# A causal 31-tap convolution stage: GpSimd makes the low halves of the weights, VectorE takes more taps

## The reference, cut to what matters

```python
def conformer_conv(x, w_in, b_in, conv_w, conv_b, ln_g, ln_b, w_out, b_out):
    a, g = jnp.split(x @ w_in + b_in, 2, axis=-1)
    h = a * jax.nn.sigmoid(g)
    h = lax.conv_general_dilated(
        h, conv_w[:, None, :], window_strides=(1,),
        padding=[(CONV_KERNEL - 1, 0)], feature_group_count=D_MODEL, ...) + conv_b
    h = jax.nn.silu(layer_norm(h, ln_g, ln_b))
    return h @ w_out + b_out
```

## Time and profile before

| | us |
|---|---|
| median of 3 runs | 1475.05 (1473.26 to 1476.8) |
| profiled execution, its own time | 1476.15 |
| span of the profiled execution | 1474.0 |
| PE busy in the span | 1447.4 (98%) |
| DVE busy | 941.6 (64%) |
| ACT busy | 627.5 (43%) |
| POOL busy | 207.2 (14%) |

### The profile page before, as it was taken

One profiled execution on the slowest core, in us unless ns is written; L12 is line 12 of the kernel. 1 busy time (PEld: TensorE's weight loads), 2 busy tenths in 40 slices (PEclk: granted clock), 3 DMA queues, 4 the chain that ended last, 5 costly groups with the idle time before them and its releaser, 6 DMA issues. The chain is left out here.

```text
span 1474.0 us, 19918 instructions
## 1 busy us (share of the span) xinstructions
PE 1447.4 (98%) x6784; PEld 1172.6 (80%) x6784; DVE 941.6 (64%) x1336; ACT 627.5 (43%) x989; POOL 207.2 (14%) x153
## 2 busy tenths in 40 slices
PE   9999999999999999999999999999889999999999
PEld 8788888888877898888888888766368888888887
DVE  7877674573646667777644646899988663544532
ACT  6444442342536665444423425777554331222210
POOL 2100000000302231000000004599512000000000
PEclk9999999999999999999999999999989999999999
DMA  5232223222322012222332332333112323222321
GB/s 187 72 100 100 100 88 127 72 100 89 119 86 72 30 58 86 97 103 86 101 113 83 103 93 93 90 112 100 60 58 94 121 91 108 86 100 96 104 93 50
DMA packets 41996, 136.99 MB, mean 93 GB/s; under 512 B 4944, under 2 KB 5456, under 8 KB 41936
## 3 DMA queue, kind: packets, MB, share of 16 engines
q1 hardware_dynamic: 40928, 133.54, 27.5%
q10 hardware_dynamic: 1008, 2.69, 0.5%
HBM read 129.85 MB, written 2.10 MB: 90 GB/s over the span
## 5 line engine op out<-in xcount | busy, mean ns | idle before, releaser
L519 PE MATMUL bank<-xh,whi 128*128 128x512 f32 x1184 | 466.8, 394 | 0.7 <-DVE res L1478 0.7
L520 PE MATMUL bank<-xl,whi 128*128 128x512 f32 x1184 | 461.0, 389 | 0.0
L521 PE MATMUL bank<-xh,wlo 128*128 128x512 f32 x1184 | 461.0, 389 | 0.0
L845 ACT ACTIVATE whi<-raw 128x1024 fp32r<-128x1024 f32 x244 | 255.7, 1050 | 232.6 <-PE bank L521 232.6
L1185 DVE TENSOR_TENSOR wlo<-raw,whi 128x1024 fp32r<-128x1024 f32 x244 | 313.9, 1286 | 47.2 <-ACT whi L845 39.9
L519 PEld LDWEIGHTS bank<-xh,whi 128*128 128x128 f32 x1184 | 222.5, 188 | 51.5 <-issue 4.2
L520 PEld LDWEIGHTS bank<-xl,whi 128*128 128x128 f32 x1184 | 222.4, 188 | 48.5 <-issue 2.7
L521 PEld LDWEIGHTS bank<-xh,wlo 128*128 128x128 f32 x1184 | 222.4, 188 | 46.4
L519 PE MATMUL bank<-ahi,whi 128*128 128x512 f32 x608 | 236.5, 389 | 0.0
L520 PE MATMUL bank<-alo,whi 128*128 128x512 f32 x608 | 236.5, 389 | 0.0
L521 PE MATMUL bank<-ahi,wlo 128*128 128x512 f32 x608 | 236.5, 389 | 0.0
(11 more groups left out here) (174 smaller groups left out, 1307.6 us busy)
## 6 DMA issues: line engine op xcount, KB each, us to landing
raw<-w_ffn_up SPq DMA_DIRECT2D x88, 512.0 KB, 3.2
raw<-w_ffn_down SPq DMA_DIRECT2D x32, 512.0 KB, 3.3
raw<-w_mlp_up SPq DMA_DIRECT2D x32, 512.0 KB, 3.2
raw<-w_mlp_down SPq DMA_DIRECT2D x32, 512.0 KB, 3.2
raw<-w_ain SPq DMA_DIRECT2D x16, 512.0 KB, 3.2
raw<-w_ffn_down SPq DMA_DIRECT2D x16, 384.0 KB, 3.1
raw<-w_qkv SPq DMA_DIRECT2D x12, 512.0 KB, 3.2
raw<-w_wo SPq DMA_DIRECT2D x8, 512.0 KB, 3.3
```

The lines of the kernel that those rows point to most:

```text
L519: nc.tensor.matmul(out_, hi, mh, start=first, stop=False)
L520: nc.tensor.matmul(out_, hi, ml, start=False, stop=False)
L521: return nc.tensor.matmul(out_, lo, mh, start=False, stop=last)
L845: nc.scalar.activation(whi[:, s, 0:tiles * P], raw[:, s, 0:tiles * P], ACT.Copy)\
```

## The change

GpSimd makes the low halves of units 4 to 16 (13 of them) that VectorE made. It does unit 2c+3 ahead of its second addition of block c (for c from 1 to 6), and unit 2c+4 ahead of its fifth (for c from 0 to 6). The taps are divided anew. In blocks 1 to 6 GpSimd has 3, 4, 4, 4, 3 and 1 taps fewer (and ScalarE as many products fewer). TensorE has two more in blocks 1 and 2. VectorE has one own tap more in block 1, and 2, 4, 4, 3 and 1 late taps more in blocks 2 to 6. VectorE still makes unit 3, and unit 17 and later.

```diff
-PE_TAPS = (8, 6, 6, 8, 8, 8, 14, 18)
+PE_TAPS = (8, 8, 8, 8, 8, 8, 14, 18)
...
-POOL_TAPS = (11, 11, 11, 11, 11, 10, 9, 5)
-LATE_TAPS = (0, 6, 10, 12, 12, 13, 8, 0)
+POOL_TAPS = (11, 8, 7, 7, 7, 7, 8, 5)
+LATE_TAPS = (0, 6, 12, 16, 16, 16, 9, 0)
 LATE_START = (2, 2, 2, 0, 0, 0, 0, 6)
...
@@ gpsimd
+            p = ph["ain"]
+
+            def split_lo(k):
+
+                s = k % SLOTS
+                pool.wait_ge(hi_done, p.unit + k + 1)
+                pool.wait_ge(lo_done, p.unit + k)
+                nc.gpsimd.tensor_tensor(wlo[:, s, :], raw[:, s, :], whi[:, s, :].bitcast(F32), ALU.subtract)\
+                    .then_inc(lo_done, 1)
+
             made = adds = 0
             for c in range(C):
                 if c >= 2:
                     pool.wait_ge(hv_ready, c - 1)
                 for k in range(1, POOL_TAPS[c]):
+                    if k == 2 and 0 < c < C - 1:
+                        split_lo(2 * c + AHEAD)
+                    if k == 5 and c < C - 1:
+                        split_lo(2 * c + 1 + AHEAD)
                     a = tapped[:, made % PARTS, :] if k == 1 else prod[:, c % 2, :]
...
@@ vector
-                split_at = [next(n for n in range(rounds) if issued[n] >= m) for m in (1, 5)]
                 gate_at = next((n for n in range(rounds) if issued[n] >= GATE_AT), rounds - 1)
                 for n in range(rounds):
-                    for j in range(2):
-                        if n == split_at[j] and c < C - 1 and (c or j):
-                            split_lo(p.unit, 0, 2 * c + j + AHEAD)
                     if n == gate_at and c < C - 1:
                         evict(c + 1, 0)
...
             collect(C - 1)
+            dve.wait_ge(lo_done, p.unit + 2 * C - 2 + AHEAD)
             split_lo(p.unit, 0, 2 * C - 2 + AHEAD)
```

## The result

| | before | after |
|---|---|---|
| median, us | 1475.05 | 1480.34 (1479.91 to 1483.07, 9 runs) |
| ratio of the runs | | 1.0042, 95% interval 1.0031 to 1.0052 |
| profiled execution, its own time | 1476.15 | 1482.14 |
| its span | 1474.0 | 1480.2 |
| from the start of `hc(0)` to the start of the last collect | 119.00 | 126.70 |

The change makes the kernel slower by 4.6 to 7.7 us; 1481.6 was forecast, 6.5 above the median before. The last row of the table is the measure that the experiments use. `hc(0)` is the first instruction of VectorE's first round. In the eleven profiles of this study it starts anywhere between 936.7 and 942.0 us, though nothing ahead of it differs but, in the last two kernels, a few small scalings on ScalarE, and a difference of spans carries that scatter.

The account below looks back on a forecast made before the run. TensorE, busy 98% of the span, was taken as the bound. Gap +6.9, clock +1.8, taps +1.7, waits -1.65, with 2.3 recovered at the end, gave +6.5 on 1475.05: 1481.6 us, range 1479.3 to 1484, wider 1478.3 to 1486.

Parts of the forecast that it names:

- The mechanism: GpSimd's queue in blocks 0 and 1: unit 5 is done only at 962.5, so TensorE's chain waits, +6.9 us.
- The price of the low half: GpSimd's subtraction of 128x1024 takes 2.4 us, range 1.9 to 2.9.
- The clock: TensorE behind the gap at unit 5: lowered clock for 3.7 us, +1.8 us.
- TensorE's taps +1.7 and the waits -1.65: Four more TensorE taps in two blocks cost 1.7 us; TensorE's waits, mostly for VectorE's collects, go, saving 1.65.
- VectorE's round: Rounds 4 to 6 with 16 late taps take about 15.3 us, under TensorE's 15.56, so VectorE stops being the bound.
- The end of the stage: Last convolution's wait for shifted copies shrinks: 2.3 of 8.75 us come back, leaving +6.5 us at the last collect.
- The sum: Whole kernel: +6.5 us on the median 1475.05 gives 1481.6; chance 0.70.
- The clock stays up: Rival: the gap at unit 5 costs 6.9 us only, +4.7 in all, 1479.8 us; chance 0.09.
- GpSimd can't keep the pace: Rival: low half over 3.4 us makes every second unit of a pair late, 1487 to 1488 us; chance 0.08.
- The lock binds the taps: Rival: the lock also binds VectorE's taps, GpSimd's additions stay at 1.64 us, +2.4 more, 1484.0 us; chance 0.06.
- Unit 5 is in time: Rival: GpSimd has unit 5 by 955.6, so the kernel gains, -2.7 us, 1472.4; chance 0.04.
- Are later units late as well?: Units behind unit 5 in GpSimd's queue: no; unit 6 done at 969, wanted after 974, later ones 1.0 us to spare.

Follow-up runs that it names:

- the last two kernels: Changed kernel with taps and places of the low halves chosen anew so that no unit is late, two variants: ratios to before 0.9975 and 0.9955.
- Experiments 1 and 2: Changed kernel, but VectorE makes the low half of unit 5 (first) or of units 4, 5 and 6 (second): ratios to before 1.0024 and 1.0005.
- Experiment 3: Changed kernel, but TensorE runs 26 matmuls that nobody reads between the chains of units 4 and 5: stage 124.53 us, ratio to before 1.0040.
- experiment 6: Changed kernel's low halves on GpSimd, but with taps divided as in the kernel before: stage 135.04 us, ratio to before 1.0114.
- Experiment 4: Changed kernel, but TensorE has 6 taps again in blocks 1 and 2 and VectorE takes the others: stage 124.97 us, ratio to before 1.0043.
- experiment 9: Changed kernel with the second new choice of taps and low-half places, so that no unit is late: stage 112.78 us, ratio to before 0.9955.
- experiment 7: Changed kernel, but VectorE's first eviction of the next block stands behind ten taps, not eight: last collect 126.53 us behind `hc(0)`, against 126.70.

## Why the prediction was right, point by point

- **The mechanism, right.** Unit 5 behind the additions of block 0 in GpSimd's queue stops TensorE. The chain of unit 5 began 15.62 us behind `hc(0)` before and 22.20 after: +6.58, forecast +6.9. Experiments 1 and 2 show that moving this unit and its neighbours takes the loss away.
- **The price of the low half, right.** 2.41 us by the rows of 128x256 and 128x512, 2.41 by the median. The estimate of 2.25 us, halved from the figure of the Trainium skill, page "GPSIMD Engine Reference", section 3.1, was 0.16 short of it.
- **The clock, right in kind and too small.** The term was +1.8, from the 3.7 us of low clock in the earlier trace rows. The low clock lasted over 5.4 us, and the term measured 8.47 - 5.69 = +2.8. Experiment 3 confirms it. I took the length from two places in the kernel before, where the level ended within 3.8 us, as the next window shows; here it held for about 6. (The idle time ahead of the first of these places, put at 3.3, is 2.97 by the rows of TensorE's matmuls; nothing else rests on it.) How long the level lasts differs from gap to gap, and whether it comes does too (experiment 6). Why stays open.

```profile
961.26 0.20 PEld L788 LDWEIGHTS bank<-shifted,dg 128*64 128x64 f32 x4 [0.35 <-issue]
```

```profile
1080.00:1084.00 4.00, 4.00 (x20) 3.25 (x19) 3.16 (x6) 3.90 (x7) 0.00 (x0) 1.00 0.00 0
```

  (The kernel before: the first load of `convolve(1)`, 5.69 us behind the chain of unit 5, and the window behind that of the earlier trace rows.)
- **TensorE's taps +1.7 and the waits -1.65, right.** From `convolve(1)` to the feature sum of block 5 it was 83.89 us before and 83.92 after, forecast +0.05. Experiment 4 shows the 1.7 by themselves.
- **VectorE's round, right, and the path through it 0.6 too short.** 15.3 was forecast, and VectorE's own round is 15.36 (experiment 9); the 15.56 measured after is TensorE's pace (experiment 7). So VectorE stopped being the bound, by 0.2 us a round. Yet `hc(7)` stood 3.1 us ahead of the feature sum of block 5, not 3.7. The first late tap starts 3.83 us behind the first load of `convolve(5)` (1031.29 to 1035.12), where 3.5 was put. From there to the collect it is 13.38 (to 1048.50), not 13.1; 0.19 of it is the eviction's wait for its chain, since experiments 7 and 9, where it does not wait, take 13.19.
- **The end of the stage.** The tail from `hc(7)` to the last collect was 15.22, forecast 15.2. The recovery was forecast as 2.3 and measured 1.7, less by the 0.6 of the point above: the feature sum of block 5 is 9.39 later relative to `hc(0)` (105.20 and 114.59), the last collect 7.70.
- **The sum.** In the stage +7.7 against +6.5: the clock 1.0 more, the recovery 0.6 less, the gap 0.3 less. By the median +5.3, which is 1.2 on the other side of the forecast. The forecast was 1.2 too low for the stage and 1.2 too high for the medians; that it lies between the two is luck. Behind the last collect both profiles take 415.1 us; what lies between the two figures is then most likely the scatter ahead of the stage, which one profile of each kernel cannot show.
- **The rivals.** *The clock stays up*: excluded. *GpSimd can't keep the pace*: excluded here, and experiment 6 shows how it looks. *The lock binds the taps*: excluded, the additions take 1.32, and those of block 0 follow each other at 1.40 (948.60 to 956.99), not 1.64. *Unit 5 is in time*: its price was wrong. The sentence "Are later units late as well?" was worked out for a TensorE already 8.7 us late. With unit 5 in time, units 6 and 7 come late, and the stage takes +2.7, not -2.7.

## What to carry to other kernels

When work moves to another engine's in-order queue, don't ask whether the engine has the time on average, but at which place of its queue each result stands and when the consumer wants it, and first of all in the start-up, where the queue is full and the lead small. When a wait is removed, work out what is late next before pricing the gain: here one unit in time brought 5.0 of 7.7 us, and the next two units, late in their turn, kept the rest. And a wait of TensorE can cost more than its length: 2.8 us more behind the 6.55 here, through the lowered clock, though nothing behind the 4.11 of experiment 6.

## What the runs showed that I had not expected

VectorE's addition of GpSimd's part (`hv<-prod,hv`, two tensors in SBUF, 0.68 us alone) took up to 2.84 us after, and up to 1.59 before. It started 0.05 us behind GpSimd's low half of unit 5 (958.21, 2.35 us):

```profile
958.26 2.84 DVE L1571 TENSOR_TENSOR hv<-prod,hv 128x512 f32<-128x512 f32 x1
```

It ended 0.5 us behind the low half, as if it had waited for all of it. In experiment 3 it was the other way round: GpSimd's low half took 2.87. The exclusive lock of which the Trainium skill speaks (page "SBUF — State Buffer", section "SBUF: two separate sides") agrees with both. That a longer GpSimd instruction makes such a meeting dearer fits the two maxima (1.59 us beside additions of 1.3, 2.84 beside the low half), but was not tested by itself.

The start of the program scatters. At the first reciprocal of 128x512 two kernels that are alike up to there stood 0.97 us apart, before and after (over all eleven profiles it starts between 46.2 and 50.9 us):

```profile
48.82 3.35 DVE L1198 RECIPROCAL rinv<-rms 128x512 f32<-128x512 f32 x1 [1.80 <-ACT rms L869]
```

```profile
47.85 3.35 DVE L1212 RECIPROCAL rinv<-rms 128x512 f32<-128x512 f32 x1 [0.85 <-ACT rms L883]
```
